# Weight sums for the seven products of a gated FFN: adding DMAs instead of GpSimd additions, with another order of splits and evacuations

## The reference, cut to what matters

```python
D_FF = 2816
# in each layer, after mixing: h is (1, 528, 1024), w_gate and w_up (1024, 2816), float32
hn = rmsnorm_2(h, ffn_norm_g)
ff = jax.nn.silu(jnp.einsum('bld,df->blf', hn, w_gate)) * jnp.einsum('bld,df->blf', hn, w_up)
return h + jnp.einsum('blf,fd->bld', ff, w_down)
```

## Time and profile before

| | |
|---|---|
| median of 3 runs | 3521.31 us (3519.25 to 3524.53) |
| the profiled execution | 3520.74 us; span of its instructions 3518.9 us |
| TensorE | busy 3138.5 us, 89% of the span; mean granted clock 0.94 |
| VectorE, ScalarE, GpSimd | busy 60%, 36%, 16% of the span |
| the four stretches of seven products | 675.7 us of the span |

### The profile page before, as it was taken

How to read it: one execution, slowest core, us unless ns; L and a number is a source line. 1 busy time by engine, 2 the same in 40 slices (tenths; PEclk the granted TensorE clock), 3 DMA queues, 4 the chain that set the end, 5 groups by cost and what they waited for, 6 DMA issues and landing times. The chain is left out here.

```text
span 3518.9 us, 52575 instructions
## 1 busy us (share of the span) xinstructions
PE 3138.5 (89%) x19600; PEld 2788.4 (79%) x19600; DVE 2119.6 (60%) x3378; ACT 1283.7 (36%) x2147; POOL 551.4 (16%) x444
## 2 busy tenths in 40 slices
PE   3999799999997998999989998779788998778887
PEld 2678778888885787888879878779788987677785
DVE  7558676546555685544444456776854346785774
ACT  3343633323223444444443323432333322443332
POOL 0000210110111002112230002322311000430421
PEclk8999899999998998999989999889999999889988
DMA  6231123223222311222221111212222111212212
GB/s 250 70 111 60 44 89 132 103 100 120 107 95 85 116 55 37 85 90 90 95 85 49 49 45 53 71 63 93 72 80 95 43 49 49 72 60 80 88 66 90
DMA packets 105701, 288.76 MB, mean 82 GB/s; under 512 B 36272, under 2 KB 36400, under 8 KB 104272
## 3 DMA queue, kind: packets, MB, share of 16 engines
q1 hardware_dynamic: 100304, 269.73, 22.8%
q0 software_dynamic: 3808, 10.38, 0.9%
q10 hardware_dynamic: 1440, 6.62, 0.5%
HBM read 284.56 MB, written 2.10 MB: 81 GB/s over the span
## 5 line engine op out<-in xcount | busy, mean ns | idle before, releaser
L343 PE MATMUL ps<-h_hi,hi_ring 128*128 128x512 f32 (+2 forms) x2672 | 872.4, 326 | 65.5 <-DVE h_lo L716 42.2
L343 PE MATMUL ps<-h_lo,hi_ring 128*128 128x512 f32 (+2 forms) x2672 | 843.6, 316 | 0.0
L343 PE MATMUL ps<-h_hi,lo_ring 128*128 128x512 f32 (+2 forms) x2672 | 840.4, 315 | 0.0
L270 DVE TENSOR_TENSOR lo_ring<-ring,hi_ring 128x1024 fp32r<-128x1024 f32 (+1 forms) x322 | 378.9, 1178 | 666.7 <-ACT hi_ring L260 665.2
L343 PEld LDWEIGHTS ps<-h_hi,hi_ring 128*128 128x128 f32 x2672 | 513.9, 192 | 127.4 <-issue 82.5
L260 ACT ACTIVATE hi_ring<-ring 128x1024 fp32r<-128x1024 f32 (+1 forms) x322 | 326.2, 1015 | 719.7 <-PE ps L343 673.4
L343 PEld LDWEIGHTS ps<-h_lo,hi_ring 128*128 128x128 f32 x2672 | 514.9, 193 | 33.6 <-issue 3.9
L343 PEld LDWEIGHTS ps<-h_hi,lo_ring 128*128 128x128 f32 x2672 | 512.3, 192 | 30.8
L2402 PE MATMUL ps<-ffn_operand,hi_ring 128*128 128x264 f32 (+1 forms) x704 | 167.9, 337 | 137.4 <-DVE arena L3421 125.2
L343 PE MATMUL ps<-hid_hi,hi_ring 128*128 128x512 f32 (+1 forms) x768 | 275.6, 359 | 3.3 <-DVE hid_lo L1087 3.3
L343 PE MATMUL ps<-hid_lo,hi_ring 128*128 128x512 f32 (+1 forms) x768 | 275.0, 358 | 0.0
(11 more groups left out here) (401 smaller groups left out, 5937.2 us busy)
## 6 DMA issues: line engine op xcount, KB each, us to landing
ring<-weights_dram SPq DMA_DIRECT2D x334, 512.0 KB, 3.3
mod_ring<-w_mod_dram SPq DMA_DIRECT2D x64, 512.0 KB, 4.4
ring<-weights_dram SPq DMA_DIRECT2D x76, 384.0 KB, 3.0
arena<-w_mod_dram SPq DMA_DIRECT2D x48, 512.0 KB, 3.4
x<-x_dram SPq DMA_DIRECT2D x1, 3072.0 KB, 16.7
arena<-c_rows_dram ACTq DMA_DIRECT2D x3, 1024.0 KB, 6.5
arena<-ret_decay_dram POOLq DMA_DIRECT2D x2, 1056.0 KB, 6.2
silu_rows<-c_rows_dram ACTq DMA_DIRECT2D x2, 1024.0 KB, 5.3
```

What stands on the lines that cost most here:

```text
L270: self.nc.vector.tensor_tensor(self.lo_ring[:, g % SPLIT, 0:w], self.ring[:, g % RING, 0:w], self.hi_ring[:, g % SPLIT, 0:w], ALU.subtract ...
L343: ins = nc.tensor.matmul(out[0:m, c:c + n], w, a[:, t0:t0 + n], start=first and k == 0 and p == 0, stop=last and k == kts - 1 and p == 2)
```

## The change

GpSimd no longer adds. For the four sums it issues four DMAs a pair (256 KB each, 176 in all), which read a quarter from DRAM again and add it to a quarter that already lies in the ring: A21 += A22 (operand 1), A11 += A21 (operand 3, once operand 0 is split), A21 += A11 (operand 2, once operand 1 is split) and A21 += A12 (operand 6, once operand 2 is split). The buffer `w_sums` goes. Raw operands 4 and 5 (A12, A22) are split in one instruction of 1024 columns; operand 6 of a pair is split in the turn of the pair itself, and the rounding and the rest of a hidden tile come in the next pair's turn. The first pair of each side is outside the hardware loop on all engines. `first_operands` splits operands 0 and 1, then 2, then 3 and the raw two.

```diff
-RAW, SUMS = {0: (0, 0), 4: (0, 1), 5: (1, 1)}, {1: 0, 2: 1, 3: 2, 6: 3}
+A11, A12, A21, A22 = (0, 0), (0, 1), (1, 0), (1, 1)
+SOURCE = {0: A11, 1: A21, 2: A21, 3: A11, 6: A21}
+SUMS = {1: (A21, A22), 3: (A11, A21), 2: (A21, A11), 6: (A21, A12)}
 EVACUATIONS = 6
...
-        slot, part = (self.g0 + (q - 3) // 2) % SPLIT, (q - 3) % 2
+        slot, part = (self.g0 + (q in (3, 6))) % SPLIT, q == 6 or q in (4, 5) and (q == 5) != self.turned_over(p)
...
+    def split(self, p, q):
+
+        if q != 4:
+            return self.ring(p, *SOURCE[q]), *self.operand(p, q)
+        first = 0 if self.turned_over(p) else (self.g0 + 2 * p) % RING
+        step = RING - 1 if self.turned_over(p) else 1
+        both = lambda ap: ap[:, self.g0 % SPLIT, :].rearrange("p (a n) -> p a n", a=2)
+        return self.core.ring[:, first:first + step + 1:step, HALF:BLOCK], both(self.core.hi_ring), both(self.core.lo_ring)
 
...
-    def add_weights(self, pool, t, n, p):
-
-
-        self.landed(pool, t, p, 0)
-        self.landed(pool, t, p, 1)
-        ring, sums = (lambda b, k: self.ring(p, b, k)), self.sums
-        tt = self.core.nc.gpsimd.tensor_tensor
-        made = lambda i: pool.wait_ge(self.made.sem, t * 8 + self.made.at(4 * n + i))
-        if n:
-            pool.wait_ge(self.lo.sem, t * 10 + self.lo.at(5 * (n - 1) + 2))
-        tt(sums[:, 0, :], ring(1, 0), ring(1, 1), ALU.add).then_inc(self.made.sem, 1)
-        made(1)
-        if n:
-            pool.wait_ge(self.lo.sem, t * 10 + self.lo.at(5 * (n - 1) + 3))
-        tt(sums[:, 1, :], sums[:, 0, :], ring(0, 0), ALU.add).then_inc(self.made.sem, 1)
-        made(2)
-        if n:
-            pool.wait_ge(self.lo.sem, t * 10 + self.lo.at(5 * (n - 1) + 4))
-        tt(sums[:, 2, :], ring(0, 0), ring(1, 0), ALU.add).then_inc(self.made.sem, 1)
-        if n:
-            pool.wait_ge(self.core.lo, t * 4 + (self.g0 + 2 * p if p else self.g0 - 2 * KT))
-        tt(sums[:, 3, :], sums[:, 1, :], ring(0, 1), ALU.add).then_inc(self.made.sem, 1)
+    def add(self, pool, n, p, q):
+
+        core, (at, added) = self.core, SUMS[q]
+        if q == 1:
+            self.landed(pool, 0, p, 1)
+        else:
+            pool.wait_ge(self.lo.sem, self.lo.at(4 * n + {3: 0, 2: 1, 6: 2}[q] + 1))
+        block, k_half = added
+        source = core.dram["weights"][core.order[self.g0 + 2 * p + block], :, k_half * HALF:(k_half + 1) * HALF]
+        pool.dma_start(self.ring(p, *at), source, accum_op=ALU.add).then_inc(self.made[q].sem, 16)
 
...
-        if q in RAW:
-            self.landed(act, t, p, RAW[q][0])
+        if q in (0, 4):
+            self.landed(act, t, p, 0)
+            if q:
+                self.landed(act, t, p, 1)
         else:
-            act.wait_ge(self.made.sem, t * 8 + self.made.at(4 * n + SUMS[q] + 1))
-        if p:
-            if q in (4, 6):
-                act.wait_ge(core.done, t * 4 + self.g0 + 2 * (p - 1) + (1 if q == 4 else 2))
-            else:
-                act.wait_ge(self.product.sem, t * 10 + self.product.at(5 * (n - 1) + min(q, 4) + 1))
-        elif q >= 3:
-            act.wait_ge(core.done, self.g0 - SPLIT + (q - 3) // 2 + 1)
+            act.wait_ge(self.made[q].sem, t * 32 + self.made[q].at(16 * (n + 1)))
+        if q in (4, 6):
+            free = self.g0 + 2 * (p - 1) + (1 if q == 4 else 2)
+            act.wait_ge(core.done, t * 4 + free)
+        elif q == 3 and not p:
+            act.wait_ge(core.done, self.g0)
         elif n:
-            act.wait_ge(self.product.sem, self.product.at(5 * (n - 1) + q + 1))
-        ins = core.nc.scalar.activation(self.operand(q)[0], self.source(p, q), ACT.Copy)
-        if q < 5:
+            act.wait_ge(self.product.sem, t * 10 + self.product.at(5 * (n - 1) + q + 1))
+        source, hi, _ = self.split(p, q)
+        ins = core.nc.scalar.activation(hi, source, ACT.Copy)
+        if q < 4:
             ins.then_inc(self.hi.sem, 1)
         else:
             ins.then_inc(core.hi, 1)
 
...
             for m in range(KT):
                 sq.add(pool, sqt, m)
-                if m == 3:
-                    sides[0].add_weights(pool, 0, 0, 0)
+                for q in {4: (1,), 5: (3, 2), 6: (6,)}.get(m, ()):
+                    sides[0].add(pool, 0, 0, q)
             for i, side in enumerate(sides):
-                if i:
-                    side.add_weights(pool, 0, H_TILES, 0)
-                tiles(pool, H_TILES - 1, 2, lambda t, n: side.add_weights(pool, t, i * H_TILES + n + 1, n + 1))
+                for p in range(H_TILES):
+                    for q in (3, 2, 6) if i or p else ():
+                        side.add(pool, i * H_TILES + p, p, q)
+                    if p < H_TILES - 1:
+                        side.add(pool, i * H_TILES + p + 1, p + 1, 1)
+                    elif not i:
+                        sides[1].add(pool, H_TILES, 0, 1)
             pool.wait_ge(f_root.sem, f_root.at(1))
             for m in range(KT):
                 sq.add(pool, sqt, m, i=KT + m)
...
+                def hidden_hi(t, i):
+                    act.wait_ge(product_ready.sem, t * 2 + product_ready.at(n0 + i + 1))
+                    nc.scalar.activation(hid[:, t * 2 + i, 0, 0:tokens], up_f[:, 0:tokens], ACT.Copy
+                                         ).then_inc(hid_done.sem, 1)
+
+                def pair(t, i, start=False, final=False):
                     following = lambda q: seven.part_hi(act, t, n0 + i + 1, i + 1, q)
                     seven.came(act, t, n0 + i, i, 0)
                     nc.scalar.activation(taken[:, 2, 0:width], seven.bank(i, 0), ACT.Copy).then_inc(seven.copied.sem, 1)
-                    for q in range(0 if final else 6):
-                        following(q)
+                    if not start:
+                        hidden_hi(t, i - 1)
+                    if not final:
+                        following(0)
+                        following(1)
+                    seven.part_hi(act, t, n0 + i, i, 6)
+                    if not final:
+                        following(2)
+                        following(3)
+                        following(4)
                     act.wait_ge(taken_in.sem, t * 2 + taken_in.at(n0 + i + 1))
                     nc.scalar.activation(sig_f[:, 0:tokens], gate_f[:, 0:tokens], ACT.Sigmoid).then_inc(sigmoid.sem, 1)
                     if final:
                         for n in range(SPLIT):
                             core.part_hi(act, 0, b0 + n_up + n)
-                    else:
-                        following(6)
-                    act.wait_ge(product_ready.sem, t * 2 + product_ready.at(n0 + i + 1))
-                    nc.scalar.activation(hid[:, t * 2 + i, 0, 0:tokens], up_f[:, 0:tokens], ACT.Copy
-                                         ).then_inc(hid_done.sem, 1)
+                        hidden_hi(t, i)
 
...
+                def hidden_lo(t, i):
+                    dve.wait_ge(hid_done.sem, t * 2 + hid_done.at(n0 + i + 1))
+                    k = t * 2 + i
+                    v.tensor_tensor(hid[:, k, 1, 0:tokens], up_f[:, 0:tokens], hid[:, k, 0, 0:tokens],
+                                    ALU.subtract).then_inc(hid_ready.sem, 1)
+
+                def pair(t, i, start=False, final=False):
                     n = n0 + i
                     g, sg, u = gate_f[:, 0:tokens], sig_f[:, 0:tokens], up_f[:, 0:tokens]
                     (g1, g2), (u1, u2) = halves(g), halves(u)
 
                     following(0)
                     following(1)
+                    seven.part_lo(dve, t, n, i, 6)
                     seven.came(dve, t, n, i, 2)
                     dve.wait_ge(seven.copied.sem, t * 2 + seven.copied.at(n + 1))
                     took(v.tensor_tensor(second, seven.bank(i, 1), taken[:, 2, 0:width], ALU.subtract))
-                    following(2)
+                    if not start:
+                        hidden_lo(t, i - 1)
                     seven.came(dve, t, n, i, 3)
                     own(1)
                     took(v.tensor_tensor(third, seven.bank(i, 3), second, ALU.add))
-                    following(3)
+                    if not start:
+                        dve.wait_ge(hid_ready.sem, t * 2 + hid_ready.at(n))
                     own(2)
                     took(v.tensor_tensor(u2, third, seven.bank(i, 2), ALU.subtract))
-                    if start:
+                    if start and not side:
                         inverse_norm()
                     seven.came(dve, t, n, i, 4)
                     took(v.tensor_tensor(g1, seven.bank(i, 0), r1, ALU.mult))
-                    following(4)
+                    following(2)
+                    following(3)
                     seven.came(dve, t, n, i, 5)
                     took(v.tensor_tensor(u1, seven.bank(i, 3), second, ALU.add))
-                    following(5)
                     seven.came(dve, t, n, i, 6)
                     took(v.tensor_tensor(g2, seven.bank(i, 2), second, ALU.subtract))
                     own(6)
```

(39 more changed lines are left out.)

53 lines of the change are left out of this document (24 added, 29 removed).

## The result

| | before | after |
|---|---|---|
| median of 4 runs each, same chip | 3520.28 us (3515.96 to 3524.53) | 3575.95 us (3571.97 to 3586.58) |
| ratio after / before, 95% interval | | 1.0163 [1.0137, 1.0189] |
| the profiled execution: span, mean granted clock | 3518.9 us, 0.94 | 3584.7 us, 0.929 |

The change made the kernel 1.6% slower. I had forecast 3463 us, so the forecast failed, also in sign; the time even lies 11 us above the range's upper end of 3565. (That end took L = 6.5.

What follows compares the result with a forecast made beforehand. A loop of waits, no engine full, bounds the kernel. At 13.8 us a pair, -16.4 (first side) - 8.8 (second) + 1.2 - 1 - 4.1 give -29.1 a layer, -58 in all: 3520.7 to near 3463 us; range 3410 to 3565.

Steps and rivals of the forecast that it cites:

- L: Time from issue to landing of the second of two adding DMAs issued in a row: 5.1 us taken, 3.3 to 6.8.
- the second bound, beat = 2L + 3.6: Turn of a pair, set by operand 2's and then operand 1's landing plus handovers: 13.8 us at L = 5.1.
- rival (a): DMAs are slow, ScalarE waits for operand 1's and 2's sums: beat 16.6, 3564 us at L = 6.5; chance 0.28.
- the forecast's own range: 3440 to 3505 us, for L from 4.6 to 5.8, rival (d) included; chance 0.50.
- the upper bound's reason: An addition also reads its destination; if that costs a second piece's share again, L = 6.8 and the beat 17.2 us.
- +0.6 into the down projection: End of each side: the first block's lo comes after both multiplications rather than before, costing 0.6 us a side.
- -1 into the second side: Start of the second side: its first `second` no longer waits for a hidden tile's rest, gaining 1 us a layer.
- Out of the output projection, -4.1 a layer: Without GpSimd's additions slowing VectorE there, TensorE's 4.09 us wait for its last block's lo goes: -4.1 us a layer.
- The table loads: Loads of 1.28 us in the first sides' loops leave with the first pair outside; if they stay, 10 us are lost.
- rival (d): GpSimd's descriptor writing costs VectorE as much as additions: 25 us more, 3488 us; its chance is within the forecast's 0.50.
- The turn without waits: Pair's turn without waits for landings, low clock: 6.68 us to g2 plus a tail of 6.57, so 13.25 us.
- Rival (b): DMAs are quick and the clock stays up: 3420 or 3391 us, 3443 with the low clock; chance 0.18.

Runs made afterwards that it cites:

- kernel 3: Changed kernel with its four DMAs a pair copying instead of adding (sums left out of the computation): 3430.17 us, one run.
- kernel 6: SyncE's gate and up loads cut to 256 of 1024 columns: 3520.49 us on the changed kernel, 3485.74 us on kernel 1, one run each.
- kernel 8: New order with GpSimd's sums and a rearranged tail, but operand 6's sum made by one adding DMA: 3435.03 us, ratio 0.9764 to the kernel before.
- kernel 1: Changed kernel with the next pair's operand 1 addition issued ahead of operand 6's: 3525.87 us, ratio 1.0025 to the kernel before.
- kernel 5: Changed kernel with each adding DMA adding only 256 of its 512 columns (other half of each sum left out): 3485.26 us, one run.

## Why the prediction was wrong

**The step that failed: "I take 5.1" for L**, in the second bound, beat = 2L + 3.6. The structure was right: the beat is two landings and their handovers. The landings measured 6.33 and 6.11, so 2 x 1.1 = +2.2 us a turn; and the handovers are 4.15, not 3.6, since GpSimd starts an issue 0.3 to 0.4 us after VectorE's end, where my sum had 0.08 once and 0.10 the other time. 13.8 + 2.2 + 0.55 = 16.55. Over 36 intervals that is 99 us more than forecast; in the trace the intervals went up by 47.6 where I had them down by 50.4, a difference of 98. It was rival (a) in its place (ScalarE's waits for operands 1 and 2) and its mechanism; I gave it 0.28. That its beat of 16.6, worked out for L = 6.5, was met with a mean L of 6.22 is luck: the handovers that were too short made up for it. (One slip of the working changed nothing here: for L = 5.8 the second bound gives 15.2 a turn and 3513 us, so the forecast's own range should have ended there and not at 3505.)

**Why L was mis-sized.** My nearest row was a plain DMA behind another one, in a quiet stretch. It left out three things. Adding doubles the engine time of a transfer (kernel 3), which I knew as the upper bound's reason and did not take. And "DMA engines are a fifth busy" was a share of before: the change itself raised it to 62%, with the ring's loads issued at the moment when operand 2's DMA is. Thin refills show 0.8 to 1.1 us of that, on each of the two landings. Third, I defined L for the second of two DMAs issued in a row. Only operand 1's is that in the changed kernel; operand 2's comes 2.5 us behind operand 3's, yet it is about as long. The last paragraph of this part says how far its neighbours account for that. The Trainium skill ("DMA: Bandwidth & Descriptors", "Rules for kernel authors") says that transfers of several issuing engines share the 16 engines and interleave; the trace agrees: SyncE's loads went to 5.0 us in the median as GpSimd's went to 5.4. The Trainium skill's formula (same page, "Anatomy of one DMA — SWDGE (gpsimd) path") gives an estimate of 2.6 us for 256 KB; no landing of 256 KB here is that short, with 2.7 the least of the plain copies and 3.6 of the additions.

**Sides' ends, +9 us a layer, not costed.** I had +0.6 into the down projection and -1 into the second side. From `second` of pair 9 (the tenth) to the first `second` of the next side it took 104.1 us instead of 93.95, and 98.9 instead of 91.2 in the second layer. Of that 1.6 and 1.4 us are the interval to the last pair's `second`, which I had put at 0. ScalarE's timeline at the start of the new side:

```profile
2448.34 0.64 ACT L2368 ACTIVATE seven_operands<-ring 128x512 fp32r<-128x512 f32 x1 [5.88 <-DMA ring<-weights_dram]
...
2457.73 0.63 ACT L2368 ACTIVATE seven_operands<-ring 128x512 fp32r<-128x512 f32 x1 [6.49 <-DMA ring<-weights_dram]
```

Landings follow each other here too: first that of operand 2 of the new side's first pair (issued at 2443.48, landed 4.8 us later), then, once it is split, that of operand 1 of the second pair (issued at 2450.53 behind operand 6's, landed 7.2 us later). TensorE is 6.7 us idle until the first `second`. I had costed the instructions of this place and not its landings.

**Out of the output projection, -4.1 a layer: about -1.4 and -0.4.** TensorE's gap of 4.09 us is gone, as said. (The second number runs from the tenth `second` of the first layer's second side; the interval to that side's last pair is 1.1 us longer, the rest 1.5 shorter.) But VectorE now waits for operand 2's sum ahead of the last block's evacuation:

```profile
2192.35 0.69 DVE L2385 TENSOR_TENSOR seven_operands<-ring,seven_operands 128x512 fp32r<-128x512 f32 x1 [2.43 <-ACT seven_operands L2368]
2192.96 0.70 DVE L793 TENSOR_TENSOR x<-ps,x 128x528 f32<-128x528 f32 x1
```

I had written that this wait lies within an output block's 5.8 us; it does not quite.

**What was right.** The second multiplication takes 0.71 for 1.69. The table loads left the loops: in the seven products there are two in all, at the sigmoid of each layer's first pair.

```profile
L3082 ACT ACT_TABLE_LOAD  x2: 1283/1283/1283, 2213.3 to 3092.7; - x2
```

GpSimd's issues do not slow VectorE, so rival (d) is out: 88 splits of 512 columns overlap an issue and no addition, and take 0.68 to 0.69 us each; the 38 wide ones take 1.22. The turn without waits is 13.1 (forecast 13.25). Rival (b) is what the kernel would be with copies: kernel 3 has its landings (3.1 to 4.1), its 3430 us (one run) lie between (b)'s 3443 for a low clock and 3391 for a high one, and so does its clock in the second side, 0.93:

```profile
2410.00:2529.00 119.00, 101.23 (x756) 99.36 (x756) 80.65 (x146) 47.69 (x81) 19.49 (x37) 0.93 0.49 158
```

So the order was costed about rightly, and the sums' price was not.

**What stays open.** How operand 2's landing of 6.1 us divides. Its DMA is issued by itself, but not to idle engines. In the 11 turns of the changed kernel in which operand 3's addition has 1.9 us or more left at that moment, operand 2 takes 6.9 us, in the other 21 it takes 5.7. (The 11 all lie in the first layer; its other five take 5.6.) So operand 3's addition just ahead goes with some 1.2 us more, and the refill issued 0.5 us behind, as kernel 6 shows, with 0.8 or more. With thin refills and little of operand 3 left it is still 4.8, against 3.6 to 4.4 for kernel 8's addition, which has no other one beside it; no run shows the cause of that rest. All this about operand 3 is read from the spread between turns: no kernel moved its DMA, or a refill, away from operand 2's, and other widths of refill were not tried. Nor was it tried to give the sums a buffer outside the ring, so that operand 2's DMA need not wait for operand 1's rest.

## What to carry to other kernels

Before moving an elementwise sum to an adding DMA, draw the chain of landings per turn: here two sums in a row on one buffer made 12.4 us of landings and 4.2 us of handovers against a turn of 15.3, and the relief of VectorE could not pay for that. Price such a DMA at twice the engine time of a copy, as measured here, and in the traffic that the change itself makes, its own neighbours in the queue included, not in that of the trace before. And measure the parts of a mixed change by themselves: the new order was worth 1.4%, and another 1.3% with a few instructions of its tail exchanged, all of it hidden behind the DMAs that came with it.

## What the runs showed of the hardware that was not expected

- An adding DMA of 256 KB from DRAM into SBUF is 144 packets and 27.2 us of engine time, a copy of the same size 80 packets and 13.4 (the bytes counted for the queue are the same, 0.26 MB each). In kernel 8, without other additions, it is 26.0 us. It lands in 4.0 us when no other addition is in flight (4.10 for operand 6 in the changed kernel, 3.99 in kernel 8), a copy in 3.1 to 3.3. Issued 0.6 us behind another it lands in 6.3 (operand 1 in the changed kernel) and 6.6 (operand 2 in kernel 1), a copy in 3.4 and 4.1.
- An issue of an adding DMA occupies GpSimd for 0.87 us (1.24 for one right behind another, which starts 0.54 after it), that of a copy for 0.54; with half the columns it is still 0.87.
- Halving the columns of such a DMA (kernel 5) leaves its 144 packets and halves its engine time, to 14.2 us. It takes 0.7 to 0.9 us off the landings of about 4.0, 2.5 off operand 1's behind operand 6's, and 0.9 off operand 2's behind operand 3's (kernel 1).
- An issue does not slow VectorE (0.68 us for a split of 512 columns beside one, as without), where a GpSimd addition makes it 1.76.
